# Prompt score steps 2 and 3, 5 and 6, 7 and 8 of an attention body, one behind the other

## What is computed

```python
s = jnp.einsum('bqhcd,bkhcd->bhcqk', q, k).astype(jnp.float32) * (DIFF_HD ** -0.5)
visible = (kpos // CHUNK)[None, :] <= (qpos // CHUNK)[:, None]
s = jnp.where(visible, s, -jnp.inf)
p = jax.nn.softmax(s, axis=-1)
a = p[:, :, 0] - lam * p[:, :, 1]
return jnp.einsum('bhqk,bkhe->bqhe', a.astype(v.dtype), v)
```

## Time and profile before

| what | value |
|---|---|
| median of three runs | 2205.0 us (2204.71 to 2205.05) |
| span of the profiled execution | 2202.9 us |
| busy, of the span | PE 99%, PEld 95%, DVE 55%, ACT 45%, POOL 39% |
| D bodies | 8, with 56 places where L823 stands |

### The profile page before, as it was taken

How to read it: one execution, slowest core, us unless ns; L and a number is a source line. 1 busy time by engine, 2 the same in 40 slices (tenths; PEclk the granted TensorE clock), 3 DMA queues, 4 the chain that set the end, 5 groups by cost and what they waited for, 6 DMA issues and landing times.

```text
span 2202.9 us, 43628 instructions
## 1 busy us (share of the span) xinstructions
PE 2188.9 (99%) x17792; PEld 2085.1 (95%) x17792; DVE 1221.9 (55%) x2107; ACT 984.6 (45%) x1898; POOL 865.4 (39%) x376
## 2 busy tenths in 40 slices
PE   7999999999999999999999999999999999999999
PEld 7888989999999999999998889899999999999999
DVE  6676666656355653266266676665563556523551
ACT  5655554445233442344246555544452234423441
POOL 4244423325334343433463354232344344434433
PEclk9999999999999999999999999999999999999999
DMA  4323222222222222321322232222222222223223
GB/s 168 98 88 93 73 95 81 79 89 70 89 78 87 87 84 75 102 97 60 106 89 92 72 112 84 79 76 70 94 78 77 96 78 96 66 85 110 80 72 112
DMA packets 82375, 193.74 MB, mean 88 GB/s; under 512 B 7584, under 2 KB 36864, under 8 KB 82176
## 3 DMA queue, kind: packets, MB, share of 16 engines
q1 hardware_dynamic: 69632, 182.41, 25.2%
q10 hardware_dynamic: 12544, 8.53, 1.2%
HBM read 177.50 MB, written 13.42 MB: 87 GB/s over the span
## 4 chain that ended last, share of the span: by engine, by line
PE 99%; ACTq 0%; issue 0%; ACT 0%; DVE 0%; DVEq 0%
PE ps L634 14%; PE ps L636 14%; PE ps L635 14%; PE ps L685 7%; PE ps L686 7%; PE ps L687 7%; PE ps L1064 4%; PE ps L1065 4%; PE ps L1063 4%; PE ps L708 2%; PE ps L664 2%; PE ps L823 2%; PE ps L858 2%; PE ps L790 2%; PE ps L782 2%; PE ps L783 1%
## 5 line engine op out<-in xcount | busy, mean ns | idle before, releaser
L511 POOL TENSOR_TENSOR wlo<-raw,whi 128x1024 fp32r<-128x1024 f32 (+1 forms) x328 | 769.2, 2366 | 1047.9 <-ACT whi L1127 1047.9
L634 PE MATMUL ps<-hl,whi 128*128 128x272 f32 x2432 | 703.7, 289 | 0.0
L636 PE MATMUL ps<-hl,wlo 128*128 128x272 f32 x2432 | 701.1, 288 | 0.0
L635 PE MATMUL ps<-hl,whi 128*128 128x272 f32 x2432 | 699.8, 288 | 0.0
L634 PEld LDWEIGHTS ps<-hl,whi 128*128 128x128 f32 x2432 | 458.5, 189 | 1.5
L636 PEld LDWEIGHTS ps<-hl,wlo 128*128 128x128 f32 x2432 | 457.5, 188 | 0.0
L635 PEld LDWEIGHTS ps<-hl,whi 128*128 128x128 f32 x2432 | 456.9, 188 | 0.0
L1127 ACT ACTIVATE whi<-raw 128x1024 fp32r<-128x1024 f32 (+1 forms) x330 | 313.4, 997 | 206.7 <-PE ps L1065 180.4
L685 PE MATMUL ps<-whi,hl 128*128 128x256 f32 x1216 | 347.9, 286 | 0.0
L686 PE MATMUL ps<-wlo,hl 128*128 128x256 f32 x1216 | 343.0, 282 | 0.0
L687 PE MATMUL ps<-whi,hl 128*128 128x256 f32 x1216 | 342.7, 282 | 0.0
(11 more groups left out here) (238 smaller groups left out, 3359.9 us busy)
## 6 DMA issues: line engine op xcount, KB each, us to landing
raw<-in_w_units_dram SPq DMA_DIRECT2D x260, 512.0 KB, 4.7
raw<-in_w_down_units_dram SPq DMA_DIRECT2D x64, 352.0 KB, 3.4
out_new_k_prompt_dram<-rawk SPq DMA_DIRECT2D x8, 512.0 KB, 3.0
out_new_v_prompt_dram<-vd SPq DMA_DIRECT2D x8, 512.0 KB, 3.0
raw<-in_w_first_dram SPq DMA_DIRECT2D x6, 512.0 KB, 5.0
kc_n<-in_cache_k_dram SPq DMA_DIRECT2D x8, 256.0 KB, 2.9
vc_n<-in_cache_v_dram SPq DMA_DIRECT2D x8, 256.0 KB, 3.3
kc_n<-in_cache_k_dram ACTq DMA_DIRECT2D x8, 256.0 KB, 4.7
```

The source lines that it names most:

```text
L511: e.tensor_tensor(wlo[:, s, a:b], raw[:, s, a:b], whi[:, s, a:b].bitcast(F32), ALU.subtract).then_inc(*S.up("w_ready", ("lo", j, part)))
L634: e.matmul(out, wh, hi, start=(c == 0), stop=False)
L635: e.matmul(out, wh, lo, start=False, stop=False)
L636: ins = e.matmul(out, wl, hi, start=False, stop=(c == KC - 1))
```

## The change

The table `FILL_SHARE` now has two numbers for each round, filling ahead of the scores and behind them, and a second table says which scores stand in which round. The sums of each round are the same but for the first two (5 and 4 pieces before, 7 and 2 now).

```diff
                     for n in range(10):
-                        if n == 0:
-                            fill(FILL_SHARE[n])
-                        if n + 2 < 10:
-                            scores(n + 2)
-                        if n:
-                            fill(FILL_SHARE[n])
+                        ahead, behind = FILL_SHARE[n]
+                        fill(ahead)
+                        for k in SCORES_AT.get(n, ()):
+                            scores(k)
+                        fill(behind)
                         weighted(n)
...
-        FILL_SHARE = (5, 4, 2, 6, 4, 5, 5, 4, 4, 1)
+        FILL_SHARE = ((7, 0), (0, 2), (0, 2), (3, 3), (0, 4), (3, 2), (0, 5), (0, 4), (0, 4), (0, 1))
+        SCORES_AT = {0: (2, 3), 2: (4,), 3: (5, 6), 5: (7, 8), 7: (9,)}
```

More of the change, by code:

```diff
@@ L1102, in program @@
                 FILL_DONE[(kind, t)] = ([-1] if end <= FILL_FIRST else []) + [
-                    n for n in range(10) if FILL_FIRST + 2 * FILL_MID + sum(FILL_SHARE[:n + 1]) >= end] + [10]
+                    n for n in range(10) if FILL_FIRST + 2 * FILL_MID + sum(map(sum, FILL_SHARE[:n + 1])) >= end] + [10]
         def filled_at(n):
```

## The result

| | before | changed |
|---|---|---|
| median, four runs each | 2205.0 us | 2232.0 us |
| lowest and highest | 2204.7, 2206.1 | 2230.7, 2241.2 |
| profiled execution: time, span | (2202.9 span) | 2241.2, 2239.4 |
| mean granted clock of the profiled execution | 1.000 | 0.992 |

The ratio is 1.013, 95% interval 1.0112 to 1.0149: slower, by 27 us against the 18.4 of the forecast. The median lies 0.02 us above the stated range.

A forecast was written before the change was run, and what follows sets the result against it. PE's matmul side, busy 2188.9 of 2202.9 us, was taken as the bound. Per body, -3 x 0.40 + 0.89 + 2.3 + 0.28 = 2.3 us, 18.4 for eight, gave 2223.4 us; eight-in-ten range 2215 to 2232.

The forecast's parts named there:

- the three places named: PE waits forecast per body: step 1's transposes 0.89 us, step 6's scores 2.3, step 6's transposes behind cached keys 0.28.
- the prediction's own signs of being wrong: No L823 wait at step 6, that wait with a shorter ACT chain, or the granted clock falling behind a wait.
- L790, which was to lose slow first pieces: Profile sign: source lines L790 and L782 should lose 24 slow first pieces in mean duration.
- Wait at the transposes of step 1: PE waits for a(1), since two more filling pieces delay step 2 and DVE's chain: 0.89 us a body.
- The start behind the release: Time PE takes to start after a releasing engine finishes: taken as 0.13 us, bounds 0 to 0.45.
- Wait at step 6: PE waits before step 6's scores for the bank pair ACT's exps(4) releases: 2.3 us a body.
- Cached keys: PE waits at step 6's transposes for ACT's copy of the cached keys: 0.28 us a body.
- Step 8: PE's wait for the bank pair exps(6) releases: 0.1 to 0.23 us, nothing in the sum, kept for the upper end.
- Saving of 0.40 a pair: Joining two score blocks saves PE changes of form: 0.40 us each, three pairs, eight bodies, 9.6 us.
- Sum: Three savings of 0.40 against waits of 0.89, 2.3 and 0.28: 2.3 us slower a body, 18.4 for eight.
- rival 3: PE's clock falls behind each of eight waits, adding 17 us: about 2240 us, chance 0.05.
- Rivals 1 and 2: Faster, waits covered, only savings count: 2195.4 us, chance 0.07; no change, shorter ACT chain, waits equal savings: 2205, chance 0.05.

The follow-up runs named there:

- The single-pair runs: Kernel before with only one pair of score steps joined: 2 and 3, 2209.0 us; 5 and 6, 2224.1 us; 7 and 8, 2205.6 us.
- the 7 and 8 run: Kernel before with only score steps 7 and 8 joined, all else as before: 2205.6 us, ratio 1.0002.
- Steps 2 and 3 in place: Kernel before with only score steps 2 and 3 joined, five and four filling pieces left in rounds 0 and 1: 2203.3 us.
- the last versions: Kernel before with steps 2, 3 and 6, 7 joined, 2197.6 us; the same with step 9 also directly behind step 8, 2195.5 us.
- the best version: Kernel before with steps 2, 3 and 6, 7 joined and step 9 directly behind step 8: 2195.5 us, ratio 0.9955.

## Why the prediction came out as it did

- **Sign, and the waits as the main mechanism: right.** PE was bound to lose what an order makes it wait; the waits came at the three places named. The single-pair runs put most of it on 5 and 6. The last of the prediction's own signs of being wrong came true, though: the granted clock fell behind a wait. And L790, which was to lose slow first pieces, went from 306 to 326 ns in the mean, since its pieces stand where the clock was low; L782 stayed (301 and 300).
- **Wait at the transposes of step 1:** forecast 0.89 us, measured 0.79 (from the last filling matmul to the first transpose 0.92, where 0.13 is usual). The start behind the release took 0.06 instead of 0.13.
- **Wait at step 6:** forecast 2.3, measured 2.3. Exps(4) ended 0.62 us later than before (157.77 - 5.41 - 151.74), forecast 0.66, and the start took 0.15.
- **Cached keys:** forecast 0.28, measured 0.27.
- **Step 8:** set at nothing, 0.12 in each body of the 7 and 8 run. I had it at 0.1 to 0.23 and pushed it into the range; it belonged in the sum.
- **Saving of 0.40 a pair:** about right. In the changed kernel the waits of 0.79, 2.3, 0.27 and 0.12 less the measured 2.46 leave 1.0 for three pairs, 0.34 each. Steps 2 and 3 in place saved 0.24 net, steps 6 and 7 in the last versions 0.75, with one more way in and out gone.
- **Sum:** 2.3 us a body forecast, 2.46 measured at the full clock; 19.7 us instead of 18.4. By the order alone the median would be 2224.7, inside the range.
- **The step that failed: the clock, put at nothing in the sum (rival 3).** I wrote "Against it: never seen since the start, but no wait of this length either", gave it 0.05, and let the forecast's range carry nothing for it. A trace without a single wait of this length was no evidence against it. It was also framed as all eight bodies or none; in the runs it is some of them, and which ones differs from run to run (granted clock 0.992, 0.996, 0.998 and 0.998, times 2241.2, 2233.0, 2230.7 and 2231.1). The price was about right in the mean (2.1 us forecast for a fall; 15.5 us in seven bodies, 2.2 each, though in fact 1.4 to 1.6 or 3.0 to 3.3), and the run with most of them met its 2240. The term, at about 7 us of the median, was missing from the sum. That the median of the four lies just outside the range, and not further, is chance: it depends on how many falls each execution had. What decides whether a body has one, and of which length, stays open. Rivals 1 and 2 fell with the wait at step 6.
- In the profiled execution the granted clock was low behind waits at step 6 and nowhere else before the last matmul. For the launch's first matmuls, which came each 0.218 us instead of 0.12, the lower level is read from their distances: the profile shows no granted clock below 1.00 there. The Trainium skill (TensorE: Matmul & The Clock Gate, Part 1) says that the throttled clock is the default and that activity releases it; by that rule an order that makes PE idle has a second price, which is what the trace shows with its 34.1 us. The Trainium skill's rule that a change of tiling mode drains TensorE (TensorEngine Tiling (Array Packing), Key Properties) is what the best version lives on, with 1.24 us less a body, but only after the waits are seen to.

## What to carry to other kernels

When TensorE has no idle time, read each wait's slack before moving work: what stands ahead of a waiting instruction is the cover of the other engine's chain, and moving it behind turns it into idle time one for one. Join two blocks only where both releases have already come, and place them by the later one. Price a new wait twice, once for its length and once for the clock that may fall behind it, and when a copy is taken out of one chain, look at what it and its follower on GpSimd will then stand beside.

## What the runs showed of the hardware

- TensorE's granted clock fell to its lower level (0.50, 1.2 instead of 2.4 GHz) behind idle stretches of about 2.2 us in seven of eight bodies of one run and two of eight of another kernel's. In the profiled executions it did not fall behind waits of 1.4 us and less (24 in the run with six pieces ahead), nor behind the eight of 1.6 us in the run with the copies behind exps(4); three further executions of that last kernel show 0.999, so one short fall each. The scatter of the time grew with the falls, from 1 us to 10.
- Some small DVE instructions were held up beside GpSimd's elementwise pass: L1891 took 2.58 us for 0.49, L1881 2.57 for 0.48, L1878 1.57 for 0.22, each beside L511. In the kernel before and in the changed one L1887 was, with 1.18 and 0.87 us for 0.15, and PE didn't wait for it. Not all were: L1885, which reads SBUF, kept its 0.15 beside L511, and what reads PSUM kept its time as well: in the changed kernel's second body L511 ran from 154.44 to 159.31, and L1859 took 0.42 there and two L1729 1.00, as without it.
- TensorE started 0.06 us behind a release by DVE (149.82 to 149.88) and 0.15 behind one by ACT (157.77 to 157.92).
